# Two uneven parts instead of two halves at the end of a transformer kernel, and twelve products moved ahead of a wait

## The reference

```python
def rmsnorm(x, g):
    y = x * lax.rsqrt(jnp.mean(x * x, axis=-1, keepdims=True) + EPS)
    return y * g
def swiglu(x, w_gate, w_up, w_down):
    return (jax.nn.silu(x @ w_gate) * (x @ w_up)) @ w_down
...
h = h + 0.5 * swiglu(rmsnorm(h, ffn2_norm[l]), ffn2_w_gate[l], ffn2_w_up[l], ffn2_w_down[l])
return rmsnorm(h, final_norm)[:, N_META:]
```

## Time and profile before

| | |
|---|---|
| median of 3 runs | 1890.07 us (1890.05 to 1890.33) |
| the profiled execution | 1890.56 us, its span 1888.4 us |
| PE busy | 1858.1 us |
| DVE, ACT, POOL busy | 1225.5, 820.8, 99.5 us |
| mean granted TensorE clock | 0.999 |

### The profile page before, as it was taken

The page is one execution under the profiler, slowest core; times in us unless marked ns, Lnnn a source line. Parts: engine busy times, 40 slices in busy tenths (PEclk is TensorE's granted clock), DMA queues, the critical chain, the costliest instruction groups (busy, mean ns, idle before and its releaser), DMA issues.

```text
span 1888.4 us, 27498 instructions
## 1 busy us (share of the span) xinstructions
PE 1858.1 (98%) x11675; PEld 1606.4 (85%) x11675; DVE 1225.5 (65%) x1498; ACT 820.8 (43%) x1154; POOL 99.5 (5%) x105
## 2 busy tenths in 40 slices
PE   8999999999999999999999999999999999999998
PEld 3788878877888888799999999888778878998998
DVE  8667743458657567587694785764554567695784
ACT  4544543336435345264452454554333354352442
POOL 0021000002000000000100100000000000110100
PEclk9999999999999999999999999999999999999999
DMA  8454423222244333222543443211122233544441
GB/s 337 154 187 157 156 80 123 89 89 68 73 123 123 98 120 95 90 74 72 139 123 107 115 121 101 90 59 46 68 83 95 90 95 95 134 112 123 116 121 66
DMA packets 66344, 208.12 MB, mean 110 GB/s; under 512 B 4512, under 2 KB 32704, under 8 KB 51376
## 3 DMA queue, kind: packets, MB, share of 16 engines
q1 hardware_dynamic: 36656, 173.55, 26.9%
q0 software_dynamic: 29568, 32.84, 8.5%
HBM read 204.27 MB, written 2.10 MB: 109 GB/s over the span
## 4 chain that ended last, share of the span: by engine, by line
PE 92%; DVE 5%; ACT 2%; issue 1%; DMA 0%; POOL 0%; DVEq 0%; ACTq 0%; POOLq 0%
PE PS L833 90%; PE PS L1000 1%; DVE W_lo L2305 1%; ACT W_hi L1675 0%; DVE N L2959 0%; ACT N L1675 0%; DVE N L2954 0%; DVE T L3037 0%; DVE N L2918 0%; DVE N L2949 0%; ACT H_hi L1675 0%; ACT X L1675 0%; DMA X<-in_xT 0%; DVE N L2333 0%; PE PS L1292 0%
## 5 line engine op out<-in xcount | busy, mean ns | idle before, releaser
L1675 ACT ACTIVATE W_hi<-W_raw 128x2048 fp32r<-128x2048 f32 (+3 forms) x158 | 289.9, 1836 | 351.4 <-PE PS L833 328.2
L833 PE MATMUL PS<-H_hi,W_hi 128*128 128x512 f32 (+2 forms) x1296 | 428.0, 345 | 5.4 <-POOL H_lo L801 2.4
L833 PE MATMUL PS<-H_lo,W_hi 128*128 128x512 f32 (+2 forms) x1296 | 425.8, 344 | 0.0
L833 PE MATMUL PS<-H_hi,W_lo 128*128 128x512 f32 (+2 forms) x1272 | 422.9, 347 | 0.0
L2305 DVE TENSOR_TENSOR W_lo<-W_raw,W_hi 128x2048 fp32r<-128x2048 f32 (+2 forms) x107 | 236.9, 2214 | 102.6 <-ACT W_hi L1675 102.4
L833 PEld LDWEIGHTS PS<-H_hi,W_hi 128*128 128x128 f32 x1296 | 236.1, 188 | 40.8 <-issue 4.4
L833 PEld LDWEIGHTS PS<-H_lo,W_hi 128*128 128x128 f32 x1296 | 235.6, 188 | 30.3 <-issue 0.7
L833 PEld LDWEIGHTS PS<-H_hi,W_lo 128*128 128x128 f32 x1272 | 232.0, 188 | 28.9 <-issue 0.7
L833 PE MATMUL PS<-G_hi,W_hi 128*128 128x264 f32 (+2 forms) x736 | 215.7, 332 | 2.1 <-DVE G_lo L3024 1.6
L833 PE MATMUL PS<-G_lo,W_hi 128*128 128x264 f32 (+2 forms) x736 | 216.2, 333 | 0.0
L833 PE MATMUL PS<-G_hi,W_lo 128*128 128x264 f32 (+2 forms) x736 | 215.6, 332 | 0.0
(11 more groups left out here) (362 smaller groups left out, 3456.7 us busy)
## 6 DMA issues: line engine op xcount, KB each, us to landing
W_raw<-in_wts SPq DMA_DIRECT2D x116, 1024.0 KB, 4.9
ring<-in_wada POOLq DMA_DIRECT2D x32, 512.0 KB, 3.9
W_raw<-in_wdown SPq DMA_DIRECT2D x12, 1024.0 KB, 5.0
W_raw<-in_wts POOLq DMA_DIRECT2D x45, 256.0 KB, 4.4
W_raw<-in_wdown SPq DMA_DIRECT2D x12, 768.0 KB, 4.4
W_raw<-in_wdown SPq DMA_DIRECT2D x12, 640.0 KB, 4.2
A_high<-in_wada SPq DMA_DIRECT2D x6, 1024.0 KB, 18.4
W_raw<-in_wdown SPq DMA_DIRECT2D x12, 384.0 KB, 4.8
```

The source lines that it names most:

```text
L833: return nc.tensor.matmul(*a, **kw)
L1675: return nc.scalar.activation(*a, **kw)
```

## The change

The halves of 256 and 256 tokens at the end become parts of 384 and 128. Part 1's inverse roots are spread into bank 5 instead of 7. In DVE's order, the scalings of part 0 are distributed anew: three, two, and then, behind the last tile of part 1, two more, the reciprocal of part 1 and the last one; before, there were four, three and one, with the reciprocal behind them. In `down_pass`, for the first pass of each FFN, the first size - 2 = 4 hidden tiles of q = 1, m = 1 (12 products) are issued ahead of the wait for `hidden_lo` rather than behind the end of q = 0.

```diff
+OUT_PARTS = (0, NB - 1, NB)
...
         def out_cols(part):
-            return slice(SEQ // 2 * part, SEQ // 2 * (part + 1))
+            return slice(OUT_PARTS[part] * P, OUT_PARTS[part + 1] * P)
...
             def out_sums(part, k):
-                for j, blk in enumerate((2 * part, 2 * part + 1)):
+                for j, blk in enumerate(range(OUT_PARTS[part], OUT_PARTS[part + 1])):
...
             def out_spread(part):
-                for blk in (2 * part, 2 * part + 1):
-                    last = mm(PS[:, 7, blk * P:(blk + 1) * P], OUT_INV[:, blk:blk + 1].to_broadcast([P, P]), ident,
+                for blk in range(OUT_PARTS[part], OUT_PARTS[part + 1]):
+                    last = mm(PS[:, (7, 5)[part], blk * P:(blk + 1) * P], OUT_INV[:, blk:blk + 1].to_broadcast([P, P]), ident,
...
             def down_last(s):
                 def tile(part, k):
-                    n, m = down_at(2, k // 2), k % 2
-                    feature_tile([(half_bank(part, k), (SEQ // 2 * part, SEQ // 2))], n % 2, m * KT * P, P, range(KT), G_hi, G_lo
+                    n, m, cols = down_at(2, k // 2), k % 2, out_cols(part)
+                    feature_tile([(half_bank(part, k), (cols.start, cols.stop - cols.start))], n % 2, m * KT * P, P, range(KT), G_hi, G_lo
...
                 begin(1)
                 products(1, 0, 0, size - 2)
+                ahead = size - 2 if part == 0 else 0
+                if ahead:
+                    products(1, 1, 0, ahead)
                 pe.wait_ge(sem("hidden_lo"), HIDDEN[name] + p1)
                 products(0, 0, size - 2, size)
                 products(0, 1, size - 2, size).then_inc(w_used, 1)
                 products(1, 0, size - 2, size)
-                products(1, 1, 0, size).then_inc(w_used, 1)
+                products(1, 1, ahead, size).then_inc(w_used, 1)
...
                 half_tile(1, 5)
-                scale(0, 0, 4)
+                scale(0, 0, 3)
                 out_square(1, 5)
                 half_tile(1, 6)
-                scale(0, 4, 7)
+                scale(0, 3, 5)
                 out_square(1, 6)
                 half_tile(1, 7)
                 dve.wait_ge(sem("residual"), RESIDUAL["down3"] + KT + KT // 2)
+                scale(0, 5, 7)
+                inverse(1)
                 scale(0, 7, KT)
-                inverse(1)
                 scale(1, 0, KT)
```

More of the change, by code:

```diff
@@ L2198, in out_norm @@
                     act.wait_ge(*n.reach("variance", part + 1))
-                    two = slice(2 * part, 2 * part + 2)
-                    activate(OUT_DEV[:, two], PS[:, 0:2, 0], ACT.Sqrt, bias=eps_rms[:, :]).then_inc(n.sem("deviation"), 1)
+                    blks = slice(OUT_PARTS[part], OUT_PARTS[part + 1])
+                    activate(OUT_DEV[:, blks], PS[:, 0:blks.stop - blks.start, 0], ACT.Sqrt, bias=eps_rms[:, :]).then_inc(n.sem("deviation"), 1)
             def pair_norm():
@@ L2825, in inverse @@
                 def inverse(part):
-                    two = slice(2 * part, 2 * part + 2)
+                    blks = slice(OUT_PARTS[part], OUT_PARTS[part + 1])
                     dve.wait_ge(*n.reach("deviation", part + 1))
-                    vector.reciprocal(OUT_INV[:, two], OUT_DEV[:, two]).then_inc(n.sem("inverse"), 1)
+                    vector.reciprocal(OUT_INV[:, blks], OUT_DEV[:, blks]).then_inc(n.sem("inverse"), 1)
                 def scale(part, k0, k1):
@@ L2833, in scale @@
                     for k in range(k0, k1):
-                        vector.scalar_tensor_tensor(out=SQ[:, k, cols], in0=n.src(k)[:, cols], scalar=n.gain(k), in1=PS[:, 7, cols],
+                        vector.scalar_tensor_tensor(out=SQ[:, k, cols], in0=n.src(k)[:, cols], scalar=n.gain(k), in1=PS[:, (7, 5)[part], cols],
                                                     op0=ALU.mult, op1=ALU.mult).then_inc(n.sem("done"), 1)
```

## The result

The changed kernel takes 1903.88 us (median of four, 1902.98 to 1904.67); the kernel before takes 1890.20 (median of four, 1890.05 to 1890.62). The ratio is 1.0071 with an interval of 1.0058 to 1.0084: 13.7 us slower, where the forecast was 4.8 slower. The profiled execution took 1904.16, with a span of 1902.0 against 1888.4. The sign held; the time lies above the range.

A forecast was written before the change was run, and what follows sets the result against it. The prediction took TensorE (PE), busy for 98% of the span, to bound the kernel. Part one's +3.8 and part two's +1.0 summed to +4.8 us, giving 1894.9 against the median of 1890.07, range 1892.0 to 1898.0.

The forecast's parts named there:

- Part two: First pass's down chunks of the three FFNs: products moved ahead of the wait on G_lo cost +1.0 us (+0.7 to +3.0).
- -0.95: First FFN: filling the gap at the G_lo wait gains 1.06 us, less 0.11 of restart.
- +0.7 and +0.9: Second and third FFN, third down chunk: later release makes PE wait on W_lo, +0.7 and +0.9 us with restarts.
- The term of 0.3 for the load chain: Next up chunk, third FFN: its load and add move back, so PE waits another 0.3 us; 0 in the second.
- rival (c): Second and third FFN: the whole load chain moves, PE waits 2.3 us instead of 0.3; 1896.9 us, chance 0.15.
- Rival (d): FFN down chunks: part two without the stall, as ACT and DVE start the third chunk sooner; 1892.0 us, chance 0.05.
- Part one: Eight final tiles and tail: parts of 384 and 128 columns cost +5.3 us in PE's stream, -1.45 in the tail: +3.8.
- rival (b): Four part 1 tiles: weight loads hide, 128-column matmuls run at streaming pace, 0.0611 us; 1890.2 us, chance 0.12.
- I take 0.11: Part 1 final tiles: a 128-column matmul takes its weight load's 0.11 us, a tile 2.64, the four together -0.8 us.
- +5.3 for PE's stream: Final tiles: 5.5 for 384 columns, -0.8 for 128 columns, +0.4 for sums, +0.2 for the spread.
- -1.45 for the tail: After tile (1,7): scaling starts earlier and is shorter, -1.65 us, last store 0.2 later; bounds -1.0 to -1.7.
- Rival (e): Four part 1 tiles: short operands slowed to four times streaming, 9.6 us on top of 4.8; 1904.5 us, chance 0.03.

The follow-up runs named there:

- part two alone: Kernel before, with only the 12 products moved ahead of the wait in all three FFNs, end still in halves: 1891.13 us, ratio 1.0005.
- part one alone: Kernel after, with nothing moved ahead of the wait, so only the parts of 384 and 128 remain: 1902.53 us, ratio 1.0066.

## Why the prediction was right and wrong

**Part two was right in its mechanism, a little off in its terms.** It gave +1.0 and alone measured +0.8, which the noise alone could give; the traces say more. The first FFN gave its -0.95 (start forecast at 519.67, found at 519.65; the edit there alone -0.93). The new waits on W_lo in the second and third FFN are 0.5 and 0.6 us, with the restart of 0.1 that makes 0.6 and 0.7, against +0.7 and +0.9. The term of 0.3 for the load chain came as some 0.4 in the third FFN of the kernel after, and not at all in that of part two alone. POOL's add DMA took 4.4 and 4.5 us in these two (1619.31 to ACT's start at 1623.73 in the kernel after), against 5.4 before: it did get shorter when it moved, so rival (c), the whole chain moving and 2.3 us of waiting, is out. Rival (d), no stalls, is out as well. In the kernel after, the final tiles start 0.88 us later than before, in part two alone 0.24; that both lie near +1.0 is in part luck, as single executions scatter by some tenths.

**Part one was right while the clock held.** 384 columns: 4.22 us a tile against 4.21. 128 columns: 2.63 against 2.64, so rival (b), hidden weight loads, is out. With 192 columns in part 1, where the clock stays up, the stretch from the first final tile (1855.81) to the last residual (1885.62) takes 29.81 us, +5.6 against a forecast of +5.3, and the tail -1.7 against -1.45: +3.9 where the text has +3.8, and +4.3 between medians. With the sums apart it is +4.3 too, at 128 columns. Together with part two's +0.8 the forecast's mechanisms come to 5.1 us; it gave 4.8.

**The failed step** is "I take 0.11 (...). Tile: 24 x 0.11 = 2.64; four ...": it took one pace for all four tiles. It holds for the first. The other three run at 0.213, 5.1 instead of 2.64 us, which is +7.5, the spreading of part 0 takes 1.25 instead of some 0.6, and the tail at half clock gains 0.8 instead of 1.7. The forecast put +5.3 for PE's stream and it was +13.5; it put -1.45 for the tail and it was -0.8. This is 8.2 + 0.7 = 8.9 us, and with part two's 0.1 less it is the 8.8 between the profiled execution (1904.16) and the forecast against its own time (1895.4).

What was left out is PE's granted clock, whose fall no term of the sum and no rival had. I read it in the windows over the tiles of before, found 1.00, and carried it over to a stream that holds something else: short tiles on both sides of twelve sums that stream one column each. The rows of before could not have given the answer, since there the same place has 256-column tiles around eight sums and the clock holds. They could have given the rival: a kernel with `keep_clock` around its last waits says that its clock can be lost. A rival with 0.213 us for the three tiles behind the sums would have added 3 x 24 x 0.10 = 7.4, and with the spreading and the tail some 1.3 more, to the 1894.9: 1903.6.

**Rival (e)** had nearly the time, 1904.5, and the wrong mechanism. It would have slowed every short matmul, the first tile included, and that one takes 2.63 us; no run shows a short matmul slowed at a granted clock of 1.00. That its time came near is luck: (e) slowed four tiles and nothing else, the chip slowed three tiles, a spreading and a tail.

The Trainium skill ("TensorE: Matmul & The Clock Gate", section "Back-to-back issue gap") gives the 56 ns that the prediction weighed for a matmul by itself, and for a stream of loads and matmuls 81 ns at 128 columns; the trace has 0.111 us. For the lower clock the section has a gap of columns / 1.2, 107 ns for 128 columns and 213 for 256. The trace agrees at 256 columns (0.213) and not at 128, where it also has 0.213. Its section "LDWEIGHTS (loading the stationary operand)" gives one figure, 107 ns for 128 columns; that agrees with the pace at the upper clock, while at the lower one the loads too start 0.213 us apart. The page's section "HAM oscillation — how this bites in real kernels" tells of a kernel with few output rows that loses the clock while it waits for data. Such waits are not the cause here: PE's records show no idle time ahead of the fall.

**What stays open.** Twelve sums in one block between 128-column tiles lost the clock in all eight executions of the kernel after and of part one alone. Tiles of 128 columns without sums among them held it (one execution), sums between 192- or 256-column tiles held it (twenty), and six and six sums between short tiles held it (ten; one execution of each kernel is profiled, the others are judged by their times and mean clocks). It isn't shown that short tiles are needed on both sides of the sums: with a wide one ahead the clock was lost in three of ten executions, with a wide one behind in the profiled one at least. The fall comes 1.2 to 2.9 us after the first sum: 1.3 in the kernel after, 2.9 in part one alone, 2.5 with the sums behind three tiles, 1.2 and 2.0 with the second and the third tile wide. What sets that, and why executions of one kernel differ, the runs don't settle. Nor was the spreading tried apart from the sums: the kernel with the sums apart moved it too.

## What to carry to other kernels

Before cutting a matmul's columns, read in a trace at what pace its weight loads follow each other: below that floor (here 0.11 us, at 192 columns as at 128) columns are free, and a cut saves nothing. Near-empty matmuls in one block between short ones can halve PE's clock without any idle time, for the price of everything behind them; spread them out, or leave all the tiles around them wide (one was not enough), and read the granted clock of the last slices whenever the order or the widths there change. Moving work ahead of a wait also moves what that work's neighbours release: move as much as fills the gap, and only where there is one.

## What the runs showed of the hardware

- Full-array matmuls with 4-byte weights at the upper clock start 0.111 us apart at 128 and at 192 columns, 0.117 to 0.118 at 256, 0.176 at 384, 0.232 at 512. At the lower clock they start 0.213 apart at 128 (kernel after) and at 256 (third tile wide).
- The granted clock fell to 0.50 with PE busy throughout, 1.3 and 2.9 us after the first of twelve one-column matmuls (1.3 us) between 128-column tiles. 72 matmuls of 128 columns held it at 1.00 for 8 us. When it was down, 78 matmuls of 128 columns in 16.7 us (three tiles and the spreading) didn't raise it; in the two kernels with a later tile of 256 columns it rose 3.1 and 1.8 us into that tile.
- One kernel (first tile wide) has two times, 1894 and 1902 us, in seven and three of ten executions, at mean clocks of 1.000 and 0.994.
- An add DMA of POOL whose start moved back by 1.6 to 2.6 us took 4.4 to 4.5 us instead of 5.4 to the release of ACT (third FFN).
